# Weight sums by accumulating DMAs in one chained buffer, pairs of neighbouring x tiles, down in two groups of four tiles, squares on ScalarE

## What is computed

```python
def rms_norm(x, g):
    y = x * rsqrt(mean(x * x, axis=-1) + 1e-6)
    return y * g

def swiglu(h, w_gate, w_up, w_down):      # 1024 -> 2816 -> 1024
    return (silu(h @ w_gate) * (h @ w_up)) @ w_down

for l in range(2):
    x = x + 0.5 * swiglu(rms_norm(x, g_ffn1[l]), w_ffn1_gate[l], w_ffn1_up[l], w_ffn1_down[l])
    h = rms_norm(x, g_mix[l])
    x = x + (conv_gating_mixer(h, ...) if l == 0 else stick_breaking_mixer(h, ...))
    x = x + 0.5 * swiglu(rms_norm(x, g_ffn2[l]), w_ffn2_gate[l], w_ffn2_up[l], w_ffn2_down[l])
return rms_norm(x, g_final)
```

## Time and profile before

| What | Value |
|---|---|
| Median of three runs | 2059.07 us |
| Profiled execution: its time | 2057.78 us |
| Profiled execution: its span | 2056.1 us |
| PE busy | 1893.6 us (92%) |
| DVE busy | 1441.8 us (70%) |
| ACT busy | 854.0 us (42%) |
| POOL busy | 744.2 us (36%) |
| Granted TensorE clock, mean | 0.956 |
| DMA read | 240.22 MB, 118 GB/s over the span |

### The profile page before, as it was taken

The page is one execution under the profiler, slowest core; times in us unless marked ns, Lnnn a source line. Parts: engine busy times, 40 slices in busy tenths (PEclk is TensorE's granted clock), DMA queues, the critical chain, the costliest instruction groups (busy, mean ns, idle before and its releaser), DMA issues.

```text
span 2056.1 us, 30552 instructions
## 1 busy us (share of the span) xinstructions
PE 1893.6 (92%) x11779; PEld 1696.5 (83%) x11779; DVE 1441.8 (70%) x1410; ACT 854.0 (42%) x1028; POOL 744.2 (36%) x551
## 2 busy tenths in 40 slices
PE   2999999989877999999599999989999969999998
PEld 2999988767657999988599998867888859999886
DVE  7778774579878778844977785453666697878642
ACT  3445442313235545522444543223555445544422
POOL 6454510331454555201645430040333274555003
PEclk6999999999988999999899999989999979999998
DMA  5788932222135888523479863223111147798321
GB/s 135 163 174 173 187 122 92 72 82 82 42 82 124 175 181 176 153 92 95 100 170 178 186 141 122 70 65 102 42 41 42 42 102 163 163 189 181 113 82 41
DMA packets 390330, 243.35 MB, mean 118 GB/s; under 512 B 13980, under 2 KB 358624, under 8 KB 390256
## 3 DMA queue, kind: packets, MB, share of 16 engines
q1 hardware_dynamic: 297088, 196.13, 32.1%
q0 software_dynamic: 93056, 46.22, 18.1%
q10 hardware_dynamic: 112, 0.03, 0.0%
HBM read 240.22 MB, written 2.10 MB: 118 GB/s over the span
## 4 chain that ended last, share of the span: by engine, by line
PE 69%; DVE 18%; issue 6%; POOL 4%; ACT 3%; DMA 0%; DVEq 0%; POOLq 0%; ACTq 0%
PE ps L360 23%; PE ps L362 22%; PE ps L361 22%; DVE w_lo L1361 5%; DVE y L1598 2%; ACT w_hi L978 2%; POOL ssq L1872 2%; POOL sq L1870 1%; PE ps L827 1%; PE ps L821 1%; DVE act_in L1397 1%; DVE xs_lo L1518 1%; DVE act_in L1402 1%; DVE x_sums L1501 1%; DVE w_lo L1332 1%
## 5 line engine op out<-in xcount | busy, mean ns | idle before, releaser
L360 PE MATMUL ps<-xs_hi,w_hi 128*128 128x256 f32 x2464 | 708.1, 287 | 110.6 <-DVE w_lo L1361 67.6
L361 PE MATMUL ps<-xs_lo,w_hi 128*128 128x256 f32 x2464 | 700.7, 284 | 0.0
L362 PE MATMUL ps<-xs_hi,w_lo 128*128 128x256 f32 x2464 | 700.4, 284 | 0.0
L1361 DVE TENSOR_TENSOR w_lo<-stage,w_hi 128x1024 fp32r<-128x1024 f32 x264 | 397.9, 1521 | 361.7 <-ACT w_hi L1051 200.8
L360 PEld LDWEIGHTS ps<-xs_hi,w_hi 128*128 128x128 f32 x2464 | 471.1, 191 | 122.3 <-DVE w_lo L1361 51.8
L361 PEld LDWEIGHTS ps<-xs_lo,w_hi 128*128 128x128 f32 x2464 | 471.4, 191 | 1.0 <-issue 1.0
L362 PEld LDWEIGHTS ps<-xs_hi,w_lo 128*128 128x128 f32 x2464 | 471.4, 191 | 0.0
L978 ACT ACTIVATE w_hi<-stage 128x1024 fp32r<-128x1024 f32 x176 | 182.7, 1057 | 306.0 <-PE ps L362 289.0
L1870 POOL TENSOR_TENSOR sq<-x_res 128x512 f32<-128x512 f32 x55 | 79.7, 1450 | 573.9 <-DVE x_res L1347 565.8
L360 PE MATMUL ps<-h_split,w_hi 128*128 128x512 f32 x704 | 278.8, 396 | 0.0
L361 PE MATMUL ps<-h_split,w_hi 128*128 128x512 f32 x704 | 278.7, 396 | 0.0
(11 more groups left out here) (229 smaller groups left out, 3024.2 us busy)
## 6 DMA issues: line engine op xcount, KB each, us to landing
stage<-in_w_ffn_gate_dram SPq DMA_DIRECT2D x176, 256.0 KB, 3.3
stage<-in_w_ffn_up_dram SPq DMA_DIRECT2D x176, 256.0 KB, 3.8
stage<-in_w_ffn_down_dram SPq DMA_DIRECT2D x176, 256.0 KB, 2.9
stage<-in_w_ffn_gate_dram POOLq DMA_DIRECT2D x88, 256.0 KB, 6.1
stage<-in_w_ffn_up_dram POOLq DMA_DIRECT2D x88, 256.0 KB, 6.8
stage<-in_w_qkv_dram SPq DMA_DIRECT2D x24, 512.0 KB, 4.9
sums<-in_w_ffn_gate_dram SPq DMA_DIRECT2D x44, 256.0 KB, 3.2
sums<-in_w_ffn_up_dram SPq DMA_DIRECT2D x44, 256.0 KB, 5.1
```

What stands on the lines that cost most here:

```text
L360: pe.matmul(to, a_hi, b_hi, start=start, stop=False, skip_group_check=True)
L361: pe.matmul(to, a_hi, b_lo, start=False, stop=False, skip_group_check=True)
L362: return pe.matmul(to, a_lo, b_hi, start=False, stop=stop, skip_group_check=True)
L1361: dve.tensor_tensor(w_lo[:, slot, :], src, w_hi[:, slot, :].bitcast(F32), ALU.subtract).then_inc(item_lo_made, 1)
```

## The change

- **Blocks.** The halves of the gate and up products are now: features in even and odd tiles, output columns in even and odd tiles, and gate and up take the place of the column halves in the scheme. A load fetches 256 neighbouring columns, so a block of 512 KB comes by one DMA with rows of 1 KB, where it took two with rows of 512 bytes.
- **Chained buffer.** A buffer chain with two halves, one for each step in turn, replaces T1 in stage and all of sums. W11 is loaded into it, then POOL issues DMAs that add the second block (T1), after T1 is split a third (T2), after T2 is split a fourth (T4). T3 is made in stage as before. POOL does no additions of weights. The items come in the order T1, W11, T3, W21, T2, W22, T4.
- **Parts of x.** Pairs are tiles (2k, 2k+1). x_pair makes the parts of the first four items, x_rest afterwards those of T2 and T4 for all four pairs.
- **Squares.** In front of an FFN, ACT squares the tiles of x into buffers (copies, act_in) behind x_rest, for FFNs 1 to 3 those of tiles 0 to 3 ahead of it; POOL only adds them up, between its DMAs. Behind the down products of FFNs 0, 2 and 3 POOL squares as before.
- **Down.** Output tiles 0 to 3 are done first over all 22 rows, then 4 to 7. An entry takes half the columns of two rows, 24 matmuls as before; hid is split again for the second group, into the places of two parts of x. x of tiles 0 to 3 is updated in the second group, at entry 13, and what follows on it (x_low, x_pair, squares) at entries 14 and 15.
- PE's down loop, POOL's gate loop, and ACT's and DVE's down loops are written out where they were loops.

```diff
-W11, W21, T1, T3, T2, W22, T4 = range(ITEMS)
+T1, W11, T3, W21, T2, W22, T4 = range(ITEMS)
+X1A, X2A, X2B, PART_S3, PART_S1, PART_S2, PART_S4 = range(7)
...
+        def gate_block(n, item, step):
+            w = ffn_weights[n][0 if item in (T3, W22) else 1]
+            odd = int(item in (W21, W22))
+            return w.rearrange("(k two p) f -> p two k f", two=2, p=P)[:, odd, :, bass.ds(step.count(2 * P, 0), 2 * P)]
...
+            def load_ffn(n):
+                for f in range(1, HF):
+                    if f > 1:
+                        sp.wait_ge(item_lo_made, lo0 + ITEMS * (f - 2) + T4 + 1)
+                        load_chain(n, Step(f))
+                    for item in (W11, T3, W21, W22):
+                        sp.wait_ge(item_lo_made, lo0 + ITEMS * (f - 1) + item + 1)
+                        load_block(n, item, Step(f))
...
             def gate_first(n):
+                pe.wait_ge(x_ready, norm * DT + GROUP)
+                for item in (W11, T1, W21, T3):
+                    pe.wait_ge(item_lo_made, n * FFN_ITEMS + item + 1)
+                    for k in range(KH - 1):
+                        pe.wait_ge(xs_lo_made, 10 * n + 2 * k + (1 if item in (W11, W21) else 2))
+                        gate_part(n, item, bank, [k])
+                pe.wait_ge(xs_lo_made, 10 * n + 2 * KH)
+                for item in range(T2):
+                    gate_part(n, item, bank, [KH - 1]).then_inc(item_used, 1)
...
+            def down_item(n, e, at):
+                part, slot = PART_S2 + e % 2, (DOWN_AT[n] + e) % RING
+                for r in range(2):
+                    cols = slice((GROUP * r + at % GROUP) * P, (GROUP * r + at % GROUP + 1) * P)
+                    mm = three(pe, ps[:, down_bank(n, at), :], w_hi[:, slot, cols], w_lo[:, slot, cols],
+                               h_hi[:, r * S:(r + 1) * S], h_lo[:, r * S:(r + 1) * S], start=(e % HF == 0 and r == 0))
...
@@ scalar engine @@
+            def gate_mid(n, step):
+                copy_r0(n, step)
+                hi(n, step, T2)
+                copy_v0(n, step)
+                hi(n, step, W22)
+                hi(n, step, T4)
+            def gate_step(n, step):
+                if not step.first():
+                    hi(n, step, T3)
+                    hi(n, step, W21)
+                gate_mid(n, step)
+                copy_v(n, step)
+                hi(n, step.next(), T1)
+                if step.first():
+                    token_rms(NORM_FFN[n], stats_bank(n))
                 hi(n, step.next(), W11)
+                silu(n, step)
...
@@ vector engine @@
             def gate_step(n, step):
+                if not step.first():
+                    lo(n, step, T3)
+                    make_hid(n, Step(step.f - 1, step.i))
+                    lo(n, step, W21)
+                lo(n, step, T2)
+                lo(n, step, W22)
+                s57(n, step)
+                lo(n, step, T4)
                 c11(n, step)
                 c22(n, step)
+                lo(n, step.next(), T1)
                 c12(n, step)
...
+                    scale_gate(n, step)
+                    lo(n, step.next(), W11)
+                    c21(n, step)
...
+            def x_rest(n):
+                for k in range(KH):
+                    dve.scalar_tensor_tensor(x_sums[:, 0, k, :], x_res[:, 2 * k, 0:HS], n1, x_sums[:, 0, k, :],
+                                             ALU.mult, ALU.add).then_inc(x_sums_made, 1)
+                for k in range(KH):
+                    dve.scalar_tensor_tensor(x_sums[:, 1, k, :], x_res[:, 2 * k + 1, 0:HS], g2, x_sums[:, 0, k, :],
+                                             ALU.mult, ALU.add).then_inc(x_sums_made, 1)
+                for q, part in enumerate((PART_S2, PART_S4)):
+                    dve.tensor_tensor(xs_lo[:, part], x_sums[:, q], xs_hi[:, part].bitcast(F32), ALU.subtract).then_inc(xs_lo_made, 1)
...
+            first_hi(1, T1)
+            first_hi(1, W11)
+            for k in range(2):
+                x_pair(1, k)
+            for j in range(GROUP):
+                x_square(1, j)
+            x_pair(1, 2)
+            first_hi(1, T3)
+            first_hi(1, W21)
+            x_pair(1, 3)
+            x_rest(1)
+            for j in range(GROUP, DT):
+                x_square(1, j)
...
@@ GpSimd @@
-            def add_t2(n, step, first=False):
-                pool.tensor_tensor(raw(T2), raw(T1), raw(W22), ALU.add).then_inc(t2_made, 1)
+            def add_t2(n, step):
+                pool.wait_ge(item_lo_made, step.count(ITEMS, n * FFN_ITEMS + T1 + 1))
+                pool.dma_start(step.chain().rearrange("p (k f) -> p k f", k=KH), gate_block(n, W22, step),
+                               accum_op=ALU.add).then_inc(t2_made, 16)
+            def add_t4(n, step):
+                pool.wait_ge(item_lo_made, step.count(ITEMS, n * FFN_ITEMS + T2 + 1))
+                pool.dma_start(step.chain().rearrange("p (k f) -> p k f", k=KH), gate_block(n, W21, step),
+                               accum_op=ALU.add).then_inc(t4_made, 16)
+            def add_first(n):
+                add_t1(n, Step(0))
+                add_t3(n, Step(0))
+                if n:
+                    for j in range(GROUP):
+                        add_square(n, j)
+                add_t2(n, Step(0))
+                add_t1(n, Step(1))
+                for j in range(GROUP if n else 0, DT):
+                    add_square(n, j)
+                add_t4(n, Step(0))
+                add_t3(n, Step(1))
+            def gate_step(n, step):
+                add_t2(n, step)
+                if step.f < HF - 1:
+                    add_t1(n, step.next())
+                add_t4(n, step)
+                if step.f < HF - 1:
+                    add_t3(n, step.next())
```

More of the change, by code:

```diff
@@ L55 @@
 RING = 4
-TAIL = [2, 3, 2, 2]
+GROUP = 4
+TAIL = 2
 RING_AT = [1, 2, 3, 0]
 DOWN_AT = [(r + 3) % RING for r in RING_AT]
[L60 to L65, removed]
+FFN_USED = GATE_ITEMS + FT - TAIL - 1
+USED0 = [FFN_USED * n for n in range(5)]
+DOWN_RAW = [6, 6, 5, 5]
+BASE = [1, 0, 1, 0]
 EVICTS = 5
@@ L392, in load, with load_block, load_chain @@
                                  src).then_inc(w_loaded[c % 2], 16)
[L394 to L412, removed]
[L414 to L417 removed]
+            def load_block(n, item, step):
+                sp.dma_start(stage[:, RAW_OF[item], :].rearrange("p (k f) -> p k f", k=KH),
+                             gate_block(n, item, step)).then_inc(raw_loaded[RAW_OF[item]], 16)
+            def load_chain(n, step):
+                sp.dma_start(step.chain().rearrange("p (k f) -> p k f", k=KH),
+                             gate_block(n, W11, step)).then_inc(chain_loaded[step.f % 2], 16)
+            def load_first(n):
+                halves = ((W11, W21), (T3, W22)) if n == 3 else ((T3, W22), (W11, W21))
+                if n == 1:
+                    sp.wait_ge(ysq_sum_made, 1)
+                elif n == 2:
+                    sp.wait_ge(item_lo_made, FFN_ITEMS + GATE_ITEMS)
+                elif n == 3:
+                    sp.wait_ge(att_summed, HEADS)
+                load_chain(n, Step(0))
                 for h, half in enumerate(halves):
@@ L424, in load_first @@
                         sp.wait_ge(item_lo_made, 2 * FFN_ITEMS - (2 if h == 0 else 0))
[L425 to L433, removed]
+                    for item in half:
+                        load_block(n, item, Step(0))
@@ L434, in load_row, with load_rows @@
+                load_chain(n, Step(1))
+            def load_rows(n, e):
+                group, pair = e // HF, e % HF
                 rows = ffn_weights[n][2].rearrange("(k p) f -> p k f", p=P)
[L435 to L438, removed]
+                sp.dma_start(stage[:, e % RING, :].rearrange("p (k f) -> p k f", k=2),
+                             rows[:, 2 * pair:2 * pair + 2, group * 512:(group + 1) * 512]).then_inc(raw_loaded[e % RING], 16)
@@ L440, in load_ffn @@
             def load_ffn(n):
+                lo0 = n * FFN_ITEMS
                 for f in range(1, HF):
[L442 to L450, removed]
@@ L1165, in _ @@
                 x_pair(0, k)
-                if k:
-                    first_hi(0, k - 1)
-            first_hi(0, 3)
+                first_hi(0, k)
+            x_rest(0)
+            for j in range(DT):
+                x_square(0, j)
             ffn(0)
```

770 lines of the change are left out of this document (382 added, 388 removed).

## The result

The changed kernel takes 2119.85 us (median of 4 runs, 2114.35 to 2121.9) against 2061.5 before (four runs of each, taken together): ratio 1.0277, 95% interval 1.0248 to 1.0306. The forecast was 1985, its range 1950 to 2055. This is rival B of the prediction, which had a chance of 0.11: the chain of accumulating DMAs sets the step.

What follows compares the result with a forecast made beforehand. PE bounds the gate/up and down loops, with losses at FFN starts, mixers and DVE's slowed subtractions. From 2057.8 us, -28 + 16 - 45 - 19 - 5 + 7 = -74 gives 1984, as median 1985; range 1950 to 2055.

Steps and rivals of the forecast that it cites:

- rival B: Gate/up steps: the same ring with L over 7.45 us makes the kernel slower than before, 2104 at L = 8; chance 0.11.
- What the chain costs: Steady gate/up steps: waiting on chained accumulating DMAs makes a step 20.3 us, costing 16 us over 40 steps; ends 0 and 180.
- 2L + 7.3: Ring length in a gate/up step: two DMA links plus 7.3 us of splits and handovers; PE doesn't wait while below 19.9.
- L: Time of one accumulating DMA link (T2 or T4) in the gate/up ring, taken as 6.5 us, between 4.8 and 8.55.
- upper bound of 8.55: Largest L for a gate/up accumulation: 5.6 plus 1.45 for twice the bytes plus 1.5 for a plain load in the way.
- two rows: Earlier trace's lone 256 KB accumulations, issued 255.61 and 110.58, taken by ACT after 4.8 and 5.6 us; basis for L.
- POOL's sums go: Steady gate/up steps: POOL's two additions and DVE's long subtractions leave, gaining 28 us; bounds 10 and 28.
- The starts: First matmuls of the four FFNs: earlier parts of x and squares on ACT gain 45 us together; bounds 15 and 75.
- The joints: After down: POOL's 9.07 us wait goes at both mixers, with some low-clock matmuls, gaining 19 us; bounds 10 and 20.
- Down: Down loops: thin cover at entries 13 to 15 costs 7 us over three FFNs; the last down window gains 5.
- The sum without the chain's loss: Whole kernel: the other terms take 90 us off 2057.8, leaving 1968 without a chain loss.
- rival with starved descriptors: GpSimd-issued DMAs starved during VectorE's two-port modes: L 7.7, step 22.7, time 2080; given 0.03 of B's chance.

Runs made afterwards that it cites:

- t4_aside: Changed kernel, but after each FFN's first step T4's accumulating DMA goes to an unread buffer and ScalarE splits T2's value instead: 2000.93 us, ratio 0.9736.
- silu_late: Changed kernel with ScalarE's silu and VectorE's product with it moved behind the split of the next T2 in every step: 2072.33 us, ratio 1.0072.
- w21_late: Changed kernel with SyncE's plain load of the next W21 issued after W22's split, behind T4's accumulation instead of ahead: 2084.08 us, ratio 1.013.
- t4_ahead: Changed kernel with POOL issuing T4's accumulation ahead of the next step's T1 accumulation instead of behind it: 2160.53 us, ratio 1.0508.

## Why the prediction was wrong

- **What the chain costs: the step that failed.** The form was right, a step as the larger of PE's 19.9 and 2L + 7.3. L was mis-sized: 6.5 us for both links, "as most plain loads come while no link of the chain runs". T2's link does take 6.1, below the value. T4's takes 9.0, since W11's, T3's and W21's loads are issued in just the 9 us between T2's and T4's, as each is released by a split of that very stretch. The mean L is 7.55, and by the prediction's formula 40 x (2 x 7.55 + 7.3 - 19.9) = 100 us instead of 16; by t4_aside the wait for T4 cost 111. That is 95 of the 135 us by which the forecast was short. The upper bound of 8.55 held this case; I chose a value near the free rows for a link whose neighbours the code names. The two rows weren't quite lone either: beside the accumulation of 255.61 two plain loads (254.53, 254.91) were still on their way, and a plain load was issued with that of 110.58 (110.61).
- **POOL's sums go, 28 us: right in kind, 20 in size.** Without the wait for T4 (t4_aside) the later steps run at 19.96, the pace of the earlier trace rows. The four long windows take 780.3 us there, against 800.8 before and 773 at the pace; what is left over lies in the second steps.
- **The starts, 45 us: 12 came.** T4 was issued 23.6 us after the mixer's end and not 19.8 (POOL's additions took 1.89 us each, not 1.3), and PE's third item of the second step began at 45.2, not 40. In the third and fourth FFN 9.6 and 0.2 came instead of 14 and 12, and the first lost 2.9 instead of gaining 9. Not seen at all was that ScalarE would meet the silu with a T2 waiting behind it. The second steps took 111.8 us in sum against 95.2, outside the window of 216 matmuls for the most part. Either change undoes it: silu_late has 94.6, and t4_aside, which leaves the silu where it was, 95.5. So it takes both the wait at the silu and the wait for T4.
- **The joints, 19 us: 28 came,** with no wait for the sum of squares. Nothing was undone there in a run, so which part gave it isn't shown.
- **Down, +7 - 5 = 2 us: 1.9 measured,** as 6 more in three loops and 4 less in the last.
- **The sum without the chain's loss** was 1968 by the prediction. t4_aside, which is that case, took 2001. By stages the starts fell 34 us short (10.8 gained, not 45) and the steady steps 7.5, while the joints gave 7 more (26, not 19) and down 2.
- **The rivals.** B's mechanism, place and break-even (L over 7.45) were as written, but its "plain load in each link" was held against two lone rows, and its chance was set by them. T2's link, the freer of the two, took 6.0 us at the least; the Trainium skill (DMA: Bandwidth & Descriptors, Anatomy of one DMA — SWDGE (gpsimd) path), weighed in the prediction, gave 3.2 for it, and here the measurement decides. T2's DMAs were issued as VectorE went on with its subtractions and took 6.0 to 7.7 us, 6.1 in the median, where the prediction's rival with starved descriptors had 7.7. The starved descriptors of the Trainium skill (SBUF — State Buffer, SBUF: two separate sides) aren't seen in these rows; no run issued the same DMA with VectorE at rest, so a smaller share isn't ruled out.

## What to carry over

When a buffer is reused for one value after the next, write down the ring (each DMA's issue to landing, each split, and what the engines do in program order between the last link and the first), and for each link list the transfers that the code releases in the stretch just before it; the latency of a lone DMA is the price of the link without them. If the ring's length is near the pace, the order of issue decides: three reorderings that left every byte as it was gave 99 us of 2120. And an engine that works in program order should stand in front of a late value only after the work that is ready.

## What the runs showed of the hardware

- T2's accumulating DMA of 512 KB in packets of 1 KB, mostly with the end of one plain load on its way at its issue and the next T1's accumulation issued 1.45 us behind it, took 6.1 us from issue to landing in the median; the earlier trace rows have 4.8 to 5.6 to the copy for 256 KB. No accumulating DMA of a block was quite alone in any run.
- The engines carried 229 GB/s with four accumulating and five plain blocks a step, at a DMA share of 1.05, without slowing PE. I had worked out 19.2 of 19.9 us for them from the earlier trace rows, near the limit.
- One plain load of 512 KB, issued 1.6 us ahead of T4's accumulation, made this 9.0 us; behind it (w21_late) or 3.05 us ahead (silu_late) it was 7.7. Putting T1's accumulation 0.75 us behind T4's instead of 7.4 us ahead (t4_ahead) left T4's at 9.3 and made T1's 11.5, from 9.2.
